# Layer 0's MLP in two passes over seven quarter products, with adaLN sums in batches of two column tiles

## The chip, the cores and the metric

The kernel runs on one core of one Trainium2 chip. The metric is the device time of one execution in microseconds (us), given as the median of three runs. The engines are named as in the profile: PE (TensorE, matmuls), DVE (VectorE), ACT (ScalarE), POOL (GpSimd) and SP (SyncE, which here only issues DMAs).

## The reference, cut to what matters

Two layers work on 1280 tokens (1024 of one sample, 256 of one prompt) of width 1024. Each layer is a mixer and then an MLP of hidden width 4096. Shift, scale and gate of every sub-layer come from a product of a conditioning vector with `ada_w` (adaLN), one vector for the sample and one for the prompt.

```python
for i in range(DEPTH):
    mod = (jax.nn.silu(cond) @ ada_w[i] + ada_b[i])[:, None, :]
    sh1, sc1, g1, sh2, sc2, g2 = jnp.split(mod, 6, axis=-1)
    h = _rms_norm(x, norm_mix[i]) * (1.0 + sc1) + sh1
    ...
    x = x + g1 * out
    h = _rms_norm(x, norm_mlp[i]) * (1.0 + sc2) + sh2
    x = x + g2 * (jnp.square(jax.nn.relu(h @ mlp_w1[i])) @ mlp_w2[i])
return _rms_norm(x, final_norm), jnp.stack(states, axis=1)
```

The mixer of layer 0 is a gated MLP over chunks beside a retention in two directions; that of layer 1 pools over windows of the sequence. The chunks of hidden columns, the passes and the quarter products below are the kernel's, the reference has only the two products.

## The kernel before

**Layout.** Activations lie transposed: 128 features on the partitions, 8 feature tiles (`DT`), 1280 tokens along the free axis in three blocks of 512, 512 and 256 (`TB`; the last is the prompt). `X` is the residual, `hH`/`hL` (layer 0) and `h1H`/`h1L` (layer 1) the normalized input of an MLP. Every operand of a product is held as a high and a low half, and `pair_pass` (L527) issues three matmuls for one product: high by high, high by low, low by high. The three matmuls of one 128 by 128 weight tile with a block of 512 tokens are called x512 below, those with the 256 tokens of the prompt or 256 columns x256, and counts are of single matmuls.

**Weights.** The hidden width is cut into 16 chunks (`NCH`) of 256 columns (`UC`). SP loads 1 MB of weights into `stage`, ACT rounds it to the high half in one of two places of `ring` (L933), POOL subtracts to get the low half (L1516). `stage` holds one load, so a next load waits for both.

**Layer 0's MLP** keeps `X` in SBUF. A chunk does its w1 product, squares the ReLU of it and adds its w2 product to `X` at once. `mlp(0, 0, first=True)` and `mlp(0, 15, last=True)` do so with plain products. Chunks 1 to 14 are a loop over `mlp_fast` (PE L2842, ACT L1247, POOL L1620, DVE L2232): the w1 product is plain (six blocks, `first_product`), the w2 product of the 1024 sample tokens uses seven products of quarter matrices for eight (`second_product`, in the order `FAST_SEQ`), and the prompt's is plain.

**Layer 1's MLP** runs in two passes, and frees SBUF for them by storing `X` to DRAM. After `plain_chunk(0)` and `(1)`, `first_pass(s, c)` (PE L2990, ACT L1391, POOL L1688, DVE L2378) handles chunks 2 to 15, chunk `2s + c`: seven quarter products for the w1 product of the sample tokens, in the order A11·B11, A12·B21, S1·G1, S2·G2, prompt 0, S3·G3, prompt 1, A22·G4, S4·B22. `G1` to `G4` are sums of quarters of the input, made once; `S1` to `S4` are sums of quarters of the weights, made in each chunk by POOL (L1674 to L1684) and split into `qsH` (ACT L1363) and `qsL` (POOL L1662). DVE adds the products (L2386: names s11, s22, s12 in the code), squares the ReLU (L2392: B11, B22, B12; `midB` and `u` in the profile) and forms the mid sums T1, T3, T2, T4 (L2368 to L2376). SP stores all of it to `mid_spill`. Then `second_pass(s)` takes two chunks at a time, loads the stored units back, and does seven quarter products again for the w2 product; `last_second` does the last two chunks plainly and finishes the tokens.

**adaLN of layer 1.** Its product with the conditioning vectors is not done on PE but as scaled sums on DVE, in the chunks of layer 0's MLP. Chunk `ch` takes batch `ch` of 16 batches; a batch has three column tiles: a load of 1.5 MB into `ada_st_mlp` (L666), and 16 DVE instructions of 128x384 (`ada_part`, L1855; two multiplications L1869, then fourteen multiply-and-adds L1872 whose two tensor inputs are the loaded tile and the running sum, both in SBUF). In the loop they come in four parts between the squares of the first blocks. In the next chunk PE transposes the sums (`ada_of_chunk`, L2767, three matmuls twice), and DVE reduces the result to columns of `mod` (L2172). While these parts run in the loop, POOL has nothing to do: its work for a chunk (weight sums L1626 to L1635, low halves) lies before and after.

**What sets the order.** Each engine's program is written out by hand, and each waits on semaphores for counts of the others'. An engine takes its instructions strictly in order; the DMA issues are in order on SP.

Of the kernel before, what the change touches and what calls it, by code (L numbers as in the profile page):

```python
# [119 lines left out]
FACTORS = {1: ("A11", "B11"), 2: ("A12", "B21"), 3: ("S4", "B22"), 4: ("A22", "T4"), 5: ("S1", "T1"), 6: ("S2", "T2"),  # L120
           7: ("S3", "T3")}
GOES_TO = {1: (0, 0), 2: (0, 0), 6: (0, 1), 5: (1, 1), 7: (1, 1), 3: (0, 1), 4: (1, 0)}
CHAIN = {6: 1, 7: 6, 4: 7, 3: 5}
FAST_SEQ = ([(1, d) for d in range(HD)] + [(2, d) for d in range(HD)]
            + [(p, d) for d0 in range(0, HD, 2) for p in (6, 5, 7, 3, 4) for d in (d0, d0 + 1)] + [("prompt", d) for d in range(DT)])
FAST_GRP = len(FAST_SEQ)
FAST_BANK = [(2, 3, 6, 1, 4, 5, 2, 3)[d] if p == "prompt" else (6, 1)[d % 2] if p in (2, 3, 5) else 2 + d for p, d in FAST_SEQ]
FAST_TILE = [(2, d) if p == "prompt" else (GOES_TO[p][1], HD * GOES_TO[p][0] + d) for p, d in FAST_SEQ]
FIRST_BANK = (0, 1, 0, 0, 0, 0)
LO_ORDER = ["B11", "B21", "T1", "T2", "B22", "T3", "T4", "p0", "p1"]  # L130
FAST_MID = len(LO_ORDER)


def earlier(seq, n):

    return max([i for i in range(n) if seq[i] == seq[n]], default=-1)


def products(l, ch):

    if not isinstance(ch, int):
        return FAST_GRP * ch + (GRP - FAST_GRP) if len(FAST[l]) else GRP * ch
    return GRP * ch + (FAST_GRP - GRP) * sum(1 for c in FAST[l] if c < ch)


def halves(l, ch):

    if not isinstance(ch, int):
        return FAST_MID * ch + (PAIRS - FAST_MID) if len(FAST[l]) else PAIRS * ch
    return PAIRS * ch + (FAST_MID - PAIRS) * sum(1 for c in FAST[l] if c < ch)  # L150


ADDS = {}
for _t, _d in BY_BLOCK:
    if _d > 0:
        ADDS[(_t, _d)] = len(ADDS)

# [2997 lines left out]
```

## Time and profile before

| | us |
|---|---|
| median of 3 runs | 2457.58 (2453.61 to 2458.58) |
| the profiled execution | 2457.45 |
| its span (first to last instruction) | 2455.5 |
| PE busy in it | 2400.2 (98%) |
| DVE busy | 1594.6 (65%) |
| POOL busy | 987.3 (40%) |
| ACT busy | 792.0 (32%) |
| mean granted TensorE clock | 0.996 of full |

Layer 0's mixer takes the first 680 us, layer 0's MLP lies from about 684 to 1511 us, layer 1's mixer up to about 1649, its MLP up to the end. In the lists of the profile a timeline row gives the start, the time of the whole row, the engine, the line, the operation with its output and inputs, how many instructions it stands for, and in brackets the idle time before and what ended it. Single matmuls are shown with their full latency (0.39 us for 512 columns) though they are issued closer together, so the pace is read from the distance of two starts.

### The profile page before, as it was taken

How to read it: one execution, taken by the hardware profiler on the slowest of the kernel's cores; microseconds unless marked ns; L12 is line 12 of the kernel's file. 1: busy time of each engine (PE TensorE's matmuls, PEld its weight loads, DVE VectorE, ACT ScalarE, POOL GpSimd, SP SyncE). 2: the span in 40 equal slices, each digit the busy share in tenths (PEclk: the TensorE clock that was granted, in tenths of full speed). 3: DMA queues.
4: the chain of work that ended last, by engine and by line, in shares of the span. 5: the costliest groups of instructions: out<-in, count | busy, mean ns of one | idle time of the engine just before them, and what ended most of it. 6: DMA issues, size and time to landing. Idle time of an engine off the chain costs nothing.

```text
span 2455.5 us, 37931 instructions
## 1 busy us (share of the span) xinstructions
PE 2400.2 (98%) x13516; PEld 2088.5 (85%) x13516; DVE 1594.6 (65%) x2600; ACT 792.0 (32%) x1234; POOL 987.3 (40%) x520
## 2 busy tenths in 40 slices
PE   8999999989999999999999999899999999999998
PEld 5988889988878888888888888778888888888887
DVE  6666832285487878877877886578333327877764
ACT  4311112151332223223223222764333334333322
POOL 0135321173023333333333333036656667776740
PEclk9999999999999999999999999999999999999999
DMA  8334523384212111221211131033343355343322
GB/s 294 121 130 153 150 91 110 121 283 157 78 60 78 60 60 60 73 89 63 74 60 60 60 102 35 18 116 124 108 141 116 132 177 217 131 146 125 121 86 86
DMA packets 156705, 274.07 MB, mean 112 GB/s; under 512 B 7716, under 2 KB 103752, under 8 KB 155720
## 3 DMA queue, kind: packets, MB, share of 16 engines
q1 hardware_dynamic: 149200, 263.22, 31.2%
q10 hardware_dynamic: 7416, 9.63, 1.4%
q8 instruction: 60, 0.98, 0.2%
q14 instruction: 29, 0.24, 0.0%
HBM read 204.66 MB, written 63.96 MB: 109 GB/s over the span
## 4 chain that ended last, share of the span: by engine, by line
PE 87%; DVE 7%; ACT 2%; issue 2%; POOL 1%; DMA 1%; SPq 0%; DVEq 0%; ACTq 0%; POOLq 0%
PE bank L527 83%; PE bank L2687 1%; PE bank L2577 1%; DMA hL_f<-in_ada_w_dram 1%; ACT yn L1136 1%; DVE X L1880 1%; DVE rst L2048 1%; DVE ada_acc_in L1872 0%; PE bank L2774 0%; DVE G1L L2357 0%; DVE ada_acc_mlp L1872 0%; DVE xgm L2080 0%; ACT pF L1186 0%; DVE h1L L2087 0%; PE bank L2636 0%
## 5 line engine op out<-in xcount | busy, mean ns | idle before, releaser
L1880 DVE SCALAR_TENSOR_TENSOR X<-bank,mod,X 128x512 f32<-128x512 f32 (+1 forms) x852 | 544.9, 683 | 232.7 <-PE bank L527 232.4
L527 PE MATMUL bank<-hH,ring 128*128 128x512 f32 (+1 forms) x2496 | 686.8, 357 | 0.5 <-DVE hL L2087 0.5
L1516 POOL TENSOR_TENSOR ring<-stage,ring 128x2048 fp32r<-128x2048 f32 x64 | 304.9, 4764 | 587.7 <-ACT ring L933 587.7
L527 PEld LDWEIGHTS bank<-hH,ring 128*128 128x128 f32 x2496 | 445.0, 189 | 66.6 <-DVE hL L2087 1.6
L527 PE MATMUL bank<-hL,ring 128*128 128x512 f32 (+1 forms) x1248 | 441.9, 354 | 0.0
L527 PEld LDWEIGHTS bank<-hL,ring 128*128 128x128 f32 x1248 | 236.2, 189 | 32.2
L527 PE MATMUL bank<-ring,hH 128*128 128x256 f32 (+1 forms) x1024 | 224.4, 315 | 3.7 <-POOL ring L1516 3.3
L933 ACT ACTIVATE ring<-stage 128x2048 fp32r<-128x2048 f32 x65 | 124.1, 1909 | 302.1 <-PE bank L527 289.8
L527 PE MATMUL bank<-midH,ring 128*128 128x256 f32 (+1 forms) x864 | 214.0, 329 | 4.3 <-DVE X L1880 4.3
L527 PE MATMUL bank<-h1H,ring 128*128 128x256 f32 (+1 forms) x864 | 209.4, 327 | 1.0 <-DVE h1L L2087 0.6
L527 PEld LDWEIGHTS bank<-ring,hH 128*128 128x128 f32 x1024 | 168.2, 192 | 15.3 <-issue 3.9
L2386 DVE TENSOR_TENSOR u<-u,bank 128x512 f32<-128x512 f32 x42 | 28.9, 688 | 213.9 <-PE bank L527 212.9
L527 PEld LDWEIGHTS bank<-midH,ring 128*128 128x128 f32 x864 | 148.3, 192 | 19.1 <-DVE X L1880 5.2
L527 PEld LDWEIGHTS bank<-h1H,ring 128*128 128x128 f32 x864 | 148.1, 190 | 17.2 <-DVE h1L L2087 1.8
L527 PE MATMUL bank<-ring,hL 128*128 128x256 f32 (+1 forms) x512 | 159.5, 312 | 0.0
L1872 DVE SCALAR_TENSOR_TENSOR ada_acc_mlp<-ada_st_mlp,sc,ada_acc_mlp 128x384 f32<-128x384 f32 (+1 forms) x266 | 149.7, 629 | 0.0
L1635 POOL TENSOR_TENSOR sumL<-sumF,sumH 128x2048 fp32r<-128x2048 f32 x14 | 64.6, 4616 | 204.2 <-DVE midF L2270 204.2
L527 PE MATMUL bank<-midL,ring 128*128 128x256 f32 (+1 forms) x432 | 141.9, 329 | 0.0
L527 PE MATMUL bank<-h1L,ring 128*128 128x256 f32 (+1 forms) x432 | 141.0, 326 | 0.0
L1699 POOL TENSOR_TENSOR ring<-stage,ring 128x1024 fp32r<-128x1024 f32 x32 | 82.9, 2601 | 56.2 <-ACT ring L1378 55.6
L527 PEld LDWEIGHTS bank<-ring,hL 128*128 128x128 f32 x512 | 98.3, 192 | 5.2
L1872 DVE SCALAR_TENSOR_TENSOR ada_acc_in<-ada_st_in,sc,ada_acc_in 128x384 f32<-128x384 f32 x112 | 98.4, 946 | 0.0
(382 smaller groups left out, 4833.6 us busy)
## 6 DMA issues: line engine op xcount, KB each, us to landing
stage<-in_mlp_w_dram SPq DMA_DIRECT2D x64, 1024.0 KB, 5.5
ada_st_mlp<-in_ada_w_dram SPq DMA_DIRECT2D x18, 1536.0 KB, 8.2
stage<-in_ev_w_in_dram SPq DMA_DIRECT2D x14, 1024.0 KB, 5.2
mid_spill<-midT SPq DMA_DIRECT2D x56, 256.0 KB, 2.2
ada_st_in<-in_ada_w_dram SPq DMA_DIRECT2D x8, 1536.0 KB, 7.2
mid_spill<-midB SPq DMA_DIRECT2D x48, 256.0 KB, 2.0
gt<-gate_spill SPq DMA_DIRECT2D x20, 256.0 KB, 3.9
x_spill<-X SPq DMA_DIRECT2D x2, 2560.0 KB, 10.5
```

The costliest lines, as they stand in the source:

```text
L527: mm = nc.tensor.matmul(out, a, b, start=first and n == 0, stop=last and n == 2, skip_group_check=chained)
L933: nc.scalar.activation(ringH[slot][:, :], stage[:, :], ACT.Copy).then_inc(w_hi, 1)
L1136: ev = nc.scalar.activation(yn[n % 2][:, d, h, :], bank[2 + 2 * (n % 2) + d][:, h * P:(h + 1) * P], ACT.Identity, scale=rmv[n % 2][:, j, 1 ...
L1516: nc.gpsimd.tensor_tensor(ringL[slot][:, :], stage[:, :], ringH[slot][:, :].bitcast(F32), ALU.subtract).then_inc(w_lo, 1)
L1635: nc.gpsimd.tensor_tensor(sumL[:, :, :], sumF[:, :, :], sumH[:, :, :].bitcast(F32), ALU.subtract).then_inc(s_lo[l], 1)
L1699: nc.gpsimd.tensor_tensor(rows_of(ringL[slot], part), rows_of(stages[c], part), rows_of(ringH[slot], part).bitcast(F32), ALU.subtract).the ...
L1872: V.scalar_tensor_tensor(out=acc, in0=src, scalar=sc2[:, k, cond:cond + 1], in1=acc, op0=ALU.mult, op1=ALU.add).then_inc(a_acc, 1)
L1880: V.scalar_tensor_tensor(out=X[:, d, cols(t)], in0=src[:, 0:TB[t][1]], scalar=gate_ap, in1=X[:, d, cols(t)], op0=ALU.mult, op1=ALU.add).th ...
L2048: e = V.bn_stats(rst[n % 2][:, HEADS * d + h, :], bank[2 + 2 * (n % 2) + d][:, h * P:(h + 1) * P])
L2386: V.tensor_tensor(buf[:, :], buf[:, :], src[:, :], ALU.add).then_inc(m_dve, 1)
L2577: mm = nc.tensor.matmul(bank[6 + d][:, h * P:(h + 1) * P], kx[j % 2][:, d, h, :], val[:, n, h * P:(h + 1) * P], start=True, stop=True)
L2687: mm = nc.tensor.transpose(tile_pair(q, j)[:, d * P:(d + 1) * P], X[:, d, n * P:(n + 1) * P], ident)
```

## The change

- Layer 0's MLP gets the structure of layer 1's: `mlp(l)` is now one function on each engine and called for both layers. `X` goes to DRAM (`x_kept`, 5 MB in two stores) and back; squared units are stored and loaded; both products use seven quarter products. In PE's program the MLP of layer 0 has 2904 x512 and 1536 x256 matmuls before, 2736 and 1536 after. The number of transposes for the sums is 96 in both.
- The inputs `B11` to `T4` of layer 0's second pass take the place of `hH`/`hL` in SBUF.
- The sums for layer 1's adaLN become 24 batches of two column tiles (1 MB, 16 DVE instructions of 128x256 each), two for each of the chunks 2 to 13. Batch `a` = 2ch−4 stands on DVE between B11 and s22, batch `b` = 2ch−3 between B22 and s12. There is one buffer for the loads, `ada_pair_st`, so a load waits for the sums of the batch before. PE turns `a` in the same chunk ahead of prompt product 1, and `b` in the next chunk ahead of S1·G1.
- POOL's program of a first-pass chunk in layer 0 is that of layer 1: weight sums, low halves, the subtractions for S1 to S4.
- Band tables and the low half of the pooling weight (`pool_weights`) are made on POOL after layer 0's last mid product; the weight has a buffer of its own.
- The tokens of layer 0's last blocks go through other SBUF places (`tile_at`), and one of them (tile 4) is turned and normalized a step earlier (`LAST_MM_AT`, `LAST_RS_AT`, `LAST_LO_AT`).

```diff
-            UA, n0, h0, p0 = U_MLP[l] + 2 * ch, PAIRS * ch, halves(l, ch), products(l, ch)
...
-        mlp(0, 0, first=True)
-        with pe.Fori(1, NCH - 1) as ch:
-            mlp_fast(0, ch)
-        mlp(0, NCH - 1, last=True)
...
+        def ada_pair_load(b):
+
+            sp.wait_ge(a_acc, ADA_OPS * (BATCHES_L0 + b))
+            sp.dma_start(ada_pair_st[:, :, :], ada_v[1][:, :, bass.ds(ADA_TILES * P * b, ADA_TILES * P)]).then_inc(a_raw, 16)
...
+            def first_stores(s, c):
+
+                ch = 2 * s + c
+                sp.wait_ge(m_dve, first_dve(l, ch) + D_AT["B11"])
+                mid_store(s, c, "B11", "B11")
+                if l == 0 and not closing(s):
+                    ada_pair_load(2 * ch - 3)
+                sp.wait_ge(m_dve, first_dve(l, ch) + D_AT["B22"])
+                mid_store(s, c, "B22", "B22")
+                if not closing(s):
+                    w1_load(ch + 2)
...
+        def ada_pair(b):
+
+            n = BATCHES_L0 + b
+            dve.wait_ge(a_raw, 16 * n + 16)
+            dve.wait_ge(a_mm, 2 * BATCHES_L0 + b)
+            for i in range(ADA_OPS):
+                k, cond = divmod(i, 2)
+                acc, src = ada_pair_acc[cond][:, :, :], ada_pair_st[:, k, :].rearrange("p (j n) -> p j n", j=ADA_TILES)
+                if k == 0:
+                    V.tensor_scalar(acc, src, sc2[:, k, cond:cond + 1], None, ALU.mult).then_inc(a_acc, 1)
+                else:
+                    dve.wait_ge(a_acc, ADA_OPS * n + i - 1)
+                    V.scalar_tensor_tensor(out=acc, in0=src, scalar=sc2[:, k, cond:cond + 1], in1=acc,
+                                           op0=ALU.mult, op1=ALU.add).then_inc(a_acc, 1)
...
+                total("s11", u1, bank[1], "2", "u1")
+                relu_squared("B11", u1)
+                if turned is not None:
+                    ada_pair_columns(turned, 1)
+                if first is not None:
+                    ada_pair(first)
+                total("s22", u5, bank[0], "7", "u5")
+                relu_squared("B22", u5)
+                if first is not None:
+                    ada_pair_columns(first, 0)
+                    ada_pair(first + 1)
...
+                total("s12", u2, bank[2], "3", "u2")
+                relu_squared("B12", u2)
...
+                quarter_product(bank[0][:, :], "S3", "G3", False)
+                if first is not None:
+                    ada_pair_turn(first, 0)
+                prompt_product(1)
+                pe.wait_ge(m_dve, d0 + D_AT["s22"])
+                quarter_product(bank[0][:, :], "A22", "G4", False)
```

**DVE.** Before, in the loop over layer 0's chunks, the sums stand between squares of the ReLU (L2237) and their low halves (L2242):

```order
L2172 TENSOR_REDUCE mod<-bank 128x3
...
L1869 TENSOR_SCALAR ada_acc_mlp<-ada_st_mlp,sc_164 128x3x128 x2
L1871 ISA
L1872 SCALAR_TENSOR_TENSOR ada_acc_mlp<-ada_st_mlp,sc_164,ada_acc_mlp 128x3x128
L1871 REGISTER_ALU
...
L2237 TENSOR_TENSOR relu_188<-relu_188 128x512
L2241 REGISTER_ALU
L2242 TENSOR_TENSOR midL<-relu_188,midH 128x512
```

After, in the first chunk of the first pass (chunk 2): the end of batch `a`, then s22 and B22, the columns, batch `b`, s12 and B12, and the mid sums:

```order
L2099 SCALAR_TENSOR_TENSOR ada_pair_acc_229<-ada_pair_st,sc_141,ada_pair_acc_229 128x256
L2189 TENSOR_TENSOR u_185<-u_185,bank 128x512
L2195 SCALAR_TENSOR_TENSOR midB_178<-u_185 128x512
L2107 TENSOR_REDUCE mod<-bank 128x2 x2
L2096 TENSOR_SCALAR ada_pair_acc_228<-ada_pair_st,sc_141 128x256
L2096 TENSOR_SCALAR ada_pair_acc_229<-ada_pair_st,sc_141 128x256
...
L2099 SCALAR_TENSOR_TENSOR ada_pair_acc_229<-ada_pair_st,sc_141,ada_pair_acc_229 128x256
L2189 TENSOR_TENSOR u_186<-u_186,bank 128x512
L2195 SCALAR_TENSOR_TENSOR u_186<-u_186 128x512
L2171 TENSOR_TENSOR midT_179<-u_186,midB_177 128x512
```

A whole batch of sums now stands ahead of s22, and another ahead of s12 and the mid sums.

**PE.** Before, the transposes of a chunk's sums stand ahead of the w1 product's first two blocks:

```order
L2905 ISA
L2769 ISA
L2774 MATMUL bank<-csm,ada_acc_mlp 128x128 x3
L2876 REGISTER_ALU
L527 MATMUL bank<-hH,ring 128x512
L527 MATMUL bank<-hL,ring 128x512
```

After, those of batch `a` stand between S3·G3 and prompt product 1 of the same chunk:

```order
L532 MATMUL bank<-G3H,hH 128x512
L532 MATMUL bank<-G3L,hH 128x512
L532 MATMUL bank<-G3H,hL 128x512
L2635 MATMUL bank<-csm,ada_pair_acc_228 128x128 x2
L2635 MATMUL bank<-csm,ada_pair_acc_229 128x128 x2
L532 MATMUL bank<-hH,ring 128x256
L532 MATMUL bank<-hL,ring 128x256
```

The turn moved from the chunk after the sums into the chunk of the sums.

**SP.** Before, the DMA issues of a chunk in layer 0's loop:

```order
L666 ISA
L666 DMA ada_st_mlp<-in_ada_w_dram 128x8x384
L253 ISA
L642 ISA
L642 DMA stage<-in_mlp_w_dram 128x8x256
L253 REGISTER_ALU
L642 ISA
L642 DMA stage<-in_mlp_w_dram 128x2x1024
```

After, those of a first-pass chunk of layer 0 (stores of units, two loads for the sums, one of weights):

```order
L805 DMA mid_spill<-midB_177 128x512
L668 ISA
L669 ISA
L669 DMA ada_pair_st<-in_ada_w_dram 128x8x256
...
L805 DMA mid_spill<-midB_178 128x512
...
L811 DMA stage<-in_mlp_w_dram 128x8x256
...
L805 DMA mid_spill<-midp 128x512
...
L805 DMA mid_spill<-midB_182 128x512
...
L669 DMA ada_pair_st<-in_ada_w_dram 128x8x256
```

The load for batch `b` (L669, its wait L668) now stands ahead of the weight load, and the one for the next chunk's batch `a` after the store of B21.

## Rows read from the trace of the kernel before

**Rows 1.** Windows: one chunk of layer 0's loop, one of layer 1's first pass.

```profile
core 0: us, PE busy (x) PEld busy (x) DVE busy (x) ACT busy (x) POOL busy (x), PEclk, DMA share, GB/s
845.57:898.67 53.10, 53.10 (x284) 45.91 (x283) 41.69 (x71) 15.09 (x21) 18.95 (x7) 1.00 0.21 69
1756.48:1781.32 24.84, 24.84 (x133) 21.52 (x133) 8.54 (x10) 8.75 (x15) 15.15 (x10) 1.00 0.37 127
```

**Rows 2.** Chain in layer 0's chunk loop: start us, us, instruction, count.

```profile
838.75 0.33 PE bank L2774 x3
839.08 5.49 PE bank L527 x24
```

**Rows 3.** Timeline, PE in chunk 0 of layer 0: start us, us, instruction, count [idle before].

```profile
719.02 0.39 PE L527 MATMUL bank<-midL,ring 128*128 128x512 f32 x1
...
719.70 0.39 PE L527 MATMUL bank<-midL,ring 128*128 128x512 f32 x1
```

**Rows 4.** Timeline, DVE in a chunk of layer 1's first pass.

```profile
1742.70 0.69 DVE L2392 SCALAR_TENSOR_TENSOR midB<-u 128x512 f32<-128x512 f32 x1
1753.04 0.69 DVE L2386 TENSOR_TENSOR u<-u,bank 128x512 f32<-128x512 f32 x1 [9.64 <-PE bank L527]
1753.76 1.38 DVE L2392 SCALAR_TENSOR_TENSOR midB<-u 128x512 f32<-128x512 f32 x1
1761.38 0.69 DVE L2386 TENSOR_TENSOR u<-u,bank 128x512 f32<-128x512 f32 x1 [6.23 <-PE bank L527]
1762.10 1.81 DVE L2392 SCALAR_TENSOR_TENSOR u<-u 128x512 f32<-128x512 f32 x1
...
1766.03 0.69 DVE L2376 TENSOR_TENSOR midT<-midB,midT 128x512 f32<-128x512 f32 x1
```

**Rows 5.** Two-tile sums, a reduction (DVE), a 1 MB load (DMA view, last figure us to landing).

```profile
17.51 5.62 DVE L1893 SCALAR_TENSOR_TENSOR ada_sum<-X,sc,ada_sum 128x256 f32<-128x256 f32 x14
L1810 DVE TENSOR_REDUCE mod<-bank 128x2 f32<-128x256 f32 x2 | 0.8, 418 | 0.0
ada_st_mlp<-in_ada_w_dram SPq DMA_DIRECT2D x1, 1024.0 KB, 5.1
```

**Rows 6.** Timeline, POOL in the chunk of rows 4.

```profile
1753.30 1.30 POOL L1682 TENSOR_TENSOR qsF<-stage 128x512 f32<-128x512 f32 x1
1754.54 1.76 POOL L1684 TENSOR_TENSOR s<-stage,qsF 128x512 f32<-128x512 f32 x1
1756.26 3.79 POOL L1662 TENSOR_TENSOR qsL<-qsF,qsH 128x512 fp32r<-128x512 f32 x3
...
1762.08 1.28 POOL L1662 TENSOR_TENSOR qsL<-s,qsH 128x512 fp32r<-128x512 f32 x1 [2.03 <-ACT qsH L1363]
```

**Rows 7.** Timeline, DVE and POOL in the mixing stage of layer 0.

```profile
334.03 11.85 DVE L1872 SCALAR_TENSOR_TENSOR ada_acc_in<-ada_st_in,sc,ada_acc_in 128x384 f32<-128x384 f32 x14
333.97 4.62 POOL L1516 TENSOR_TENSOR ring<-stage,ring 128x2048 fp32r<-128x2048 f32 x1 [36.73 <-ACT ring L933]
...
353.91 7.49 DVE L1872 SCALAR_TENSOR_TENSOR ada_acc_in<-ada_st_in,sc,ada_acc_in 128x384 f32<-128x384 f32 x14
356.90 8.88 POOL L1516 TENSOR_TENSOR ring<-stage,ring 128x2048 fp32r<-128x2048 f32 x1 [18.31 <-ACT ring L933]
```

**Rows 8.** Timeline, POOL beside the sums of a chunk of layer 0's loop.

```profile
1125.51 4.62 POOL L1635 TENSOR_TENSOR sumL<-sumF,sumH 128x2048 fp32r<-128x2048 f32 x1 [14.59 <-DVE midF L2270]
```

**Rows 9.** Timeline, POOL: first and last piece of the band tables.

```profile
1485.74 0.70 POOL L1585 MEMSET bandT<- 128x144 f32 x4
...
1497.89 0.10 POOL L1612 MEMSET band_edge<- 128x1 f32 x1
```

**Rows 10.** Waits of PE over the whole span: total us, times, longest us.

```profile
PE bank L527 <- DVE X L1880: 5.1, 4, 2.3
PE bank L527 <- POOL ring L1699: 2.1, 1, 2.1
PE bank L527 <- DVE G4L L2357: 2.0, 1, 2.0
```

**Rows 11.** Timeline of PE, and window, at the end of layer 0's MLP.

```profile
1509.37 0.39 PE L527 MATMUL bank<-midH,ring 128*128 128x256 f32 x1 [2.26 <-DVE X L1880]
1509.00:1513.00 4.00, 3.63 (x18) 3.63 (x19) 2.46 (x6) 0.00 (x0) 4.00 (x1) 0.59 0.00 0
```

More of the change, by code:

```diff
@@ L112 @@
 END_DVE_AT = {10: [0], 12: [1], 14: [2], 16: [3], 18: [4], 20: [5], 21: [6], 23: [7, 8, 9]}
-FAST = [range(1, NCH - 1), range(0)]
 HD = DT // 2
[L120 to L156, printed above, removed]
 SLOT_END = NT - 2
@@ L373, in build @@
     cd = small("cd", [P, 8])
+    dead_kb = off[0]
     vmv = small("vmv", [P, NT * 4, 2])
@@ new lines, in build, with held @@
+    F_KB = {"B11": 0, "p": 8, "B21": 40, "T2": 48, "T1": 24, "T3": 32, "B22": 64, "T4": 72}
+    QUARTER = {"B11": (0, 0, 0), "p": (0, 1, 0), "B21": (1, 0, 0), "T2": (1, 1, 0), "T1": (0, 1, 1), "B22": (1, 1, 1)}
+    def held(name, full, i):
+        m = ((hH_f, hL_f) if full else (hH, hL))[1 if name == "T4" else 0 if name == "T3" else QUARTER[name][0]]
+        if name in ("T3", "T4"):
+            return m[:, HD * i:HD * (i + 1), 1024:T]
+        _, half, tb = QUARTER[name]
+        return m[:, HD * half + 2 * i:HD * half + 2 * i + 2, 512 * tb:512 * (tb + 1)]
@@ L1492, in _ @@
-        for i in (1, 2, 3, 4):
-            sum2_hi(0, i, (1,))
-        mid_high(0, "T1")
-        mid_high(0, "T3")
-        second_pass(0)
-        with act.Fori(1, NSUP - 2) as s:
-            second_pass(s)
-        second_pass(NSUP - 2, plain=True)
-        act.wait_ge(m2_mm[1], M2_END)
-        w2_high(NSUP - 1, 0, 1)
-        w2_high(NSUP - 1, 1, 1)
-        mid_high(NSUP - 1, "B22")
+        mlp(1)
         for j in range(NT):
@@ L1770, in _ @@
[L1770 to L1777 removed]
+        mlp(1)
     @block.vector
@@ L2452, in _ @@
-        mid_low(0, "T2")
-        second_pass(0)
-        with dve.Fori(1, NSUP - 2) as s:
-            second_pass(s)
-        second_pass(NSUP - 2, plain=True)
-        mid_low(NSUP - 1, "T1", 3)
-        mid_low(NSUP - 1, "B22", 4)
+        mlp(1)
         for i, (t, d) in enumerate(BY_LAST):
@@ L2647, in _ @@
                     (state_keys, state_values)[half_of](ADVANCE[n])
-            if ui - 1 in ADA_IN_UNITS and ui < FIRST_GATE and not (kind == "u" and half == 1):
+            if ui - 1 in ADA_IN_UNITS and ui <= VAL_FIRST and not (kind == "u" and half == 1):
                 if ui == 5:
@@ L2720, in pool_tile @@
             else:
-                pe.wait_ge(gain_ok, 6) if j else pe.wait_ge(relu_ok[0], NTB * HT * NCH)
+                after(pe, gain_ok, 6 if j else 0)
             tile_in(2, j)
```

1771 lines of the change are left out of this document (766 added, 1005 removed).

## The prediction

> **What bounds the kernel now.** I looked first at PE, which is busy for 98% of the span, and then at the two stages that the change concerns, by windows. In one chunk of layer 0's loop PE is busy for all of the 53.10 us, and in one chunk of layer 1's first pass for all of its 24.84 us [rows 1]. So today both stages run at PE's pace, and whatever PE no longer issues is gained, as long as DVE and POOL keep up. How much room they have is in the same rows: in layer 1's chunk DVE is busy for 8.54 us and POOL for 15.15. The sums of adaLN are what has to be fitted in there. The reader is to see in the DVE rows of that chunk the two gaps in which they will lie: 9.64 us ahead of s22 and 6.23 us ahead of s12, both waits for PE [rows 4].
>
> **What is removed.** PE issues 2904 − 2736 = 168 matmuls of 512 columns fewer. Three of them take 719.70 − 719.02 = 0.68 us [rows 3], 0.2267 us each, so 168 are 38.1 us. The x256 and the transposes stay the same in number. The loop of before gives nothing more back, since PE has no idle time in it [rows 1]. If PE bounds everything in the new layer 0 too, the time is 2457.45 − 38.1 = 2419.4 us.
>
> **The pace of PE in the new chunk.** The first pass of layer 0 has layer 1's matmuls (24.84 us) and twice four transposes. Three transposes take 839.08 − 838.75 = 0.33 us [rows 2], eight 0.88. So PE alone would need 24.84 + 0.88 = 25.7 us for each of the 12 chunks with sums.
>
> **The chain on DVE.** A multiply-and-add of 128x256 takes 5.62 / 14 = 0.40 us [rows 5], a batch of 16 is 6.4 us. There is one buffer, so the load of batch b starts only when a's sums have read it: 5.1 us to landing for 1 MB [rows 5], and I add an estimated 0.5 us for SP to notice and DVE to go on, 5.6 in all. s22, B22 and two reductions lie under it (0.69 + 0.69 + 2 × 0.42 = 2.2 us [rows 4, 5]). One round of the chunk is then: s11 and B11 1.4; two reductions 0.8; batch a 6.4; load of b 5.6; batch b 6.4; s12, B12 and four mid sums 4.2 (from 1761.38 to 1766.72 are 5.34 us, of which B12 took 1.12 longer than the 0.69 of B11 [rows 4]). The sum is 24.8 us, just under PE's 25.7. The next chunk's batch a has 6.4 us for its load, enough for 5.6. If DVE were alone, the sums would thus cost PE nothing.
>
> **What POOL adds.** DVE is not alone. The rows of layer 1's chunk show B22 at 1.38 us and B12 at 1.81 where B11 takes 0.69 [rows 4], each beside a subtraction on POOL that began just before or with it, and POOL's L1684 takes 1.76 where its like takes 1.30 [rows 6]. In layer 0's mixing stage it is clearer: fourteen multiply-and-adds that take 7.49 us in one place take 11.85 beside one POOL instruction of 4.62, that is 4.4 longer; and a POOL instruction that starts inside the 7.49 takes 8.88 instead of 4.62, 4.3 longer [rows 7]. So a DVE instruction with two inputs in SBUF and a POOL instruction do not run together, they add up. DVE instructions that read PSUM (L2386, 0.69 in every row) are not held up. The loop of before kept out of this: POOL is idle for 14.59 us around the sums [rows 8]. The new place does not: POOL has its work in every first-pass chunk, and the sums are at both of its halves.
>
> So I add up what cannot overlap in one chunk. DVE: 28 multiply-and-adds × 0.40 = 11.2; B11, B22, B12 2.1; four mid sums 2.6 (the 5.34 us above without s12, B12 and the wait behind it); together 15.9. (The four multiplications, with one SBUF tensor, I count as free.) POOL: 15.15 less the hindrance of 0.46 in L1684 = 14.7 [rows 1, 6]. The sum is **30.6 us** against PE's 25.7: this is the lower bound, if POOL is packed into every moment that DVE leaves free. The upper one follows from where those moments are. Of DVE's 24.8 us, 8.9 are free, but most in pieces of 0.7 to 0.8 us (s11, s22, s12, reductions, multiplications), shorter than any POOL instruction of 1.3; only the load's 5.6 us less B22 is a long one. If POOL gets only these 4.9 us, the chunk takes 24.8 + 14.7 − 4.9 = **34.6 us**. I take 33.0, nearer to the upper end, because a POOL instruction that overhangs a short piece holds DVE for its rest, and because PE's own waits leave some time unused by both.
>
> The page "SBUF — State Buffer" of the Trainium skill ("Who interferes with whom") has the same as a rule: a DVE instruction with two SBUF inputs and a GpSimd instruction that reads SBUF need one shared port, and who starts first holds it for the whole instruction. By it alone POOL would get in between any two of DVE's, and the chunk would be near 34.6. The row with 8.88 us speaks against that half of it, since there a stream of DVE instructions held POOL off until its end; by this the chunk would be near 30.6.
>
> The stall is thus 33.0 − 25.7 = 7.3 us in each of 12 chunks, **+88 us**. It shows at PE's turn of batch a, ahead of prompt product 1. Queued behind DVE's sums are s22, B22, s12 and the mid sums, and for those wait A22·G4 and the next S1·G1 on PE, the stores and the weight load on SP. Chunks 14 and 15 have no sums and keep 24.84.
>
> **The rest of the change.** The stores and loads of X and units are those of layer 1, whose chunk has a DMA share of 0.37 [rows 1]; with 2 MB for the sums I expect no DMA bound: from 0 to +5 us. The second pass is a copy of layer 1's: its start there costs PE waits of 2.0 and 2.1 us [rows 10], and these come; the wait of 2.26 at the end of layer 0's MLP [rows 11] and one for X goes (5.1 us in four, 2.3 the longest [rows 10]). I count 0, from −4 to +4. The band tables take 1498.0 − 1485.74 = 12.3 us of POOL [rows 9]. They now come after POOL's last mid product, after the last split of weights, while PE has the plain closing products of layer 0: 192 x512, 192 × 0.2267 = 43.5 us. That is their cover; half of them uncovered would be +6, so 0, up to +6. Tile 4 a step earlier is 0 to −1.
>
> **Sum.** 2457.45 − 38.1 + 88 + 0 = **2507 us**. The profiled execution (2457.45, its span 2455.5 and 2 us around it) is practically the median of the runs (2457.58).
>
> **Rivals.**
> *A, the other side: DVE and POOL fit.* Mechanism: POOL's instructions fall into DVE's free 8.9 us and DVE's into POOL's pauses, or the interference binds less with 0.40 us instructions than with those I read. The chunk stays at PE's 25.7 and the time is 2419; each us above costs 12. It decides at a chunk of 25.7 + 38.1 / 12 = 28.9 us: below, the change wins. For it: mid sums and sums of 128x256 without POOL beside them run unhindered. Against: the bound of 30.6 is only arithmetic on what rows 7 show. Chance 0.17, of it 0.13 below 2450.
> *B, packed.* Streams of DVE hold POOL off, and POOL catches up in the load and in PE's time. 30.6 us, stall 4.9 × 12 = 59, time 2478. Chance 0.28.
> *C, alternating and slower still.* 34.6 us, 8.9 × 12 = 107, time 2526; and PE's pauses may cost clock: after one of 2.26 us the window shows a granted clock of 0.59, about half of 2.4 GHz for most of 4 us [rows 11]. Such a window costs about 0.41 × 4 = 1.6 us, in 12 chunks 20 us, if PE has no slack behind the turn: 2546. Chance 0.20.
> *D, not what it says.* PE's second pass of layer 0 waits for loads or splits, or the load of b is late on SP behind the store of B11: up to some 2 us in each of 7 rounds beside any of the others. Chance 0.03 by itself.
> My forecast between B and C has 0.32.
>
> A page of the Trainium skill, "TensorE: Matmul & The Clock Gate" (Why this matters for your kernels), has it that idle gaps between bursts of matmuls bring the half rate; the row with 0.59 agrees, and that is the second half of rival C.
>
> **The numbers.** Range: A beyond its upper part (0.13) and the far end of C (0.05) are left out, so from 2440 to 2545. A measurement of this kernel can tell about 0.2% (5 us) from no change. Faster than 2452.5: 0.15. Within: 0.05. Slower: 0.80.
>
> **What the profile after would show.** Matmuls of `pair_pass` fewer by 168. Distance between SP's weight loads in layer 0's first pass: 33 us (25.7 by A, 30.6 by B, 34.6 by C). Idle time of PE of about 7 us before the first transposes of each chunk, released by the sums, and next to none there by A. The mean of a two-tile multiply-and-add well above 0.48 us, and POOL's L1674 to L1684 and L1516 of layer 1's kind longer in layer 0 than in layer 1. Layer 0's second pass at the pace of layer 1's. I would be wrong if the multiply-and-adds show their 0.48 beside busy POOL rows, or if PE waits for something else than the sums.

## The result

The changed kernel takes 2544.49 us (median of 4 runs, 2540.73 to 2546.89), the one before 2455.92 in the same comparison. The ratio is 1.036, with an interval from 1.0341 to 1.0379. That is 88.6 us slower. The forecast was 2507 in a range from 2440 to 2545, so the direction and the mechanism were right and the loss was 1.8 times the one forecast (49.6). The median lies 0.5 us inside the range and two of the four runs lie above it, so that the range held is luck. The profiled execution has a span of 2539.0 us, and its mean granted clock fell from 0.996 to 0.974.

The pace of layer 0's first pass is read from SP's weight loads, one for each chunk (timeline of SP after the change, start and duration in us first):

```profile
862.48 0.41 SPq L811 DMA_DIRECT2D stage<-in_mlp_w_dram  x1
...
899.21 0.41 SPq L811 DMA_DIRECT2D stage<-in_mlp_w_dram  x1
...
936.25 0.41 SPq L811 DMA_DIRECT2D stage<-in_mlp_w_dram  x1
```

The three stand 36.73 and 37.04 us apart; over 12 chunks, from 717.98 to 1154.52 us, the mean is 36.38. PE alone needs 25.72, as a run below shows. Where PE waits, over the whole span of the changed kernel:

```profile
PE bank L2635 <- DVE ada_pair_acc L2099: 96.1, 11, 10.8
...
PE bank L532 <- DVE u L2189: 9.3, 1, 9.3
```

96.1 us are waits ahead of the turn of batch a, in 11 places (8.7 us each), that is in every chunk with sums but the first. Each looks like this one in PE's timeline:

```profile
897.24 1.09 PE L2635 MATMUL bank<-csm,ada_pair_acc 128*128 128x128 f32 x4 [8.40 <-DVE ada_pair_acc L2099]
```

The forecast said to look at DVE and POOL beside each other. First DVE in one chunk of the changed kernel's first pass (the batch a before it ends at 896.9; 903.29 is b, 916.99 is the next a):

```profile
896.92 0.67 DVE L2189 TENSOR_TENSOR u<-u,bank 128x512 f32<-128x512 f32 x1
...
902.76 0.62 DVE L2096 TENSOR_SCALAR ada_pair_acc<-ada_pair_st,sc 128x256 f32<-128x256 f32 x2 [3.50 <-DMA ada_pair_st<-in_ada_w_dram]
903.29 5.63 DVE L2099 SCALAR_TENSOR_TENSOR ada_pair_acc<-ada_pair_st,sc,ada_pair_acc 128x256 f32<-128x256 f32 x14
909.03 0.69 DVE L2189 TENSOR_TENSOR u<-u,bank 128x512 f32<-128x512 f32 x1
909.75 1.81 DVE L2195 SCALAR_TENSOR_TENSOR u<-u 128x512 f32<-128x512 f32 x1
...
916.99 17.08 DVE L2099 SCALAR_TENSOR_TENSOR ada_pair_acc<-ada_pair_st,sc,ada_pair_acc 128x256 f32<-128x256 f32 x14
933.99 0.67 DVE L2189 TENSOR_TENSOR u<-u,bank 128x512 f32<-128x512 f32 x1
```

Then POOL in the same stretch:

```profile
909.73 1.29 POOL L1565 TENSOR_TENSOR hL<-s,hH 128x512 fp32r<-128x512 f32 x1 [13.01 <-ACT hH L1253]
917.62 1.39 POOL L1577 TENSOR_TENSOR hL_f<-stage 128x512 f32<-128x512 f32 x1 [6.61 <-PE bank L532]
920.44 1.59 POOL L1581 TENSOR_TENSOR hL_f<-hL_f,stage 128x512 f32<-128x512 f32 x1 [1.43 <-PE bank L532]
921.99 4.79 POOL L1451 TENSOR_TENSOR ring<-stage,ring 128x2048 fp32r<-128x2048 f32 x1
926.73 1.45 POOL L1585 TENSOR_TENSOR hL_f<-stage 128x512 f32<-128x512 f32 x1
928.14 1.44 POOL L1587 TENSOR_TENSOR s<-stage,hL_f 128x512 f32<-128x512 f32 x1
929.55 4.25 POOL L1565 TENSOR_TENSOR hL<-hL_f,hH 128x512 fp32r<-128x512 f32 x3
```

The reader is to see three things. Batch b takes 5.63 us for its fourteen multiply-and-adds, the 0.40 each of [rows 5]. Batch a takes **17.08** for the same fourteen. And POOL has nearly its whole work of the chunk, eight of nine instructions, from 917.62 to 933.80, inside batch a; it is idle under the load of b (896.92 to 902.76) and under batch b.

The first chunk with sums shows the same program with another timing. There PE came late to S1·G1 (the 9.3 us of wait for s11 above), so POOL's block, which waits for that product, was released only when most of batch a was done. The batch takes 5.63 us, and PE has no wait at its turn (DVE's and POOL's timeline):

```profile
739.05 5.63 DVE L2099 SCALAR_TENSOR_TENSOR ada_pair_acc<-ada_pair_st,sc,ada_pair_acc 128x256 f32<-128x256 f32 x14
743.08 2.75 POOL L1577 TENSOR_TENSOR hL_f<-stage 128x512 f32<-128x512 f32 x1 [6.77 <-PE bank L532]
```

Windows of the changed kernel: behind the turn, a whole chunk, and layer 0's second pass.

```profile
899.00:903.00 4.00, 4.00 (x20) 4.00 (x20) 0.51 (x2) 0.00 (x0) 0.00 (x0) 0.50 1.02 349
899.21:936.25 37.04, 28.61 (x141) 24.89 (x141) 32.81 (x47) 8.75 (x14) 16.03 (x9) 0.87 0.41 141
1180.00:1500.00 320.00, 317.88 (x1707) 276.01 (x1706) 232.33 (x264) 115.80 (x142) 227.40 (x131) 1.00 0.44 156
```

The clock is 0.50 behind PE's pause, the chunk has PE busy for 28.61 of 37.04 us (against 24.84 of 24.84 in [rows 1]), and the second pass runs at PE's pace with 317.88 of 320.

### The profile page after: what moved, and what is told of

It is laid out like the page before. It is cut to its first block, busy times and chain, and to the rows that moved or that the text cites. A ratio compares the mean times of both kernels' runs of the same rounds, so it can differ in the third digit from the quotient of the medians.

```text
span 2539.0 us, 37580 instructions
## 1 busy us (share of the span) xinstructions
PE 2386.4 (94%) x13348; PEld 2078.1 (82%) x13348; DVE 1665.8 (66%) x2457; ACT 836.9 (33%) x1299; POOL 1211.5 (48%) x702
## 3 DMA queue, kind: packets, MB, share of 16 engines
q1 hardware_dynamic: 196128, 337.68, 38.1%
## 4 chain that ended last, share of the span: by engine, by line
PE 78%; DVE 10%; issue 8%; ACT 2%; DMA 1%; POOL 1%; SPq 0%; DVEq 0%; ACTq 0%; POOLq 0%
PE bank L532 73%; DVE ada_pair_acc L2099 2%; PE bank L2548 1%; DVE G1L L2160 1%; PE bank L2436 1%; PE bank L2845 1%; DMA hL_f<-in_ada_w_dram 1%; DVE G1F L2137 1%; ACT yn L1151 1%; POOL ring L1602 1%; DVE rst L1967 0%; PE bank L2635 0%; DVE G3F L2140 0%; DVE xgm L1999 0%; DVE h1L L2006 0%
## 5 line engine op out<-in xcount | busy, mean ns | idle before, releaser
L532 PE MATMUL bank<-hH,ring 128*128 128x256 f32 (+1 forms) x2856 | 650.6, 337 | 4.2 <-POOL ring L1602 3.0
L1799 DVE SCALAR_TENSOR_TENSOR X<-bank,mod,X 128x512 f32<-128x512 f32 (+1 forms) x576 | 373.9, 686 | 280.0 <-PE bank L532 277.9
L1451 POOL TENSOR_TENSOR ring<-stage,ring 128x2048 fp32r<-128x2048 f32 x47 | 223.7, 4759 | 289.0 <-ACT ring L946 289.0
L2099 DVE SCALAR_TENSOR_TENSOR ada_pair_acc<-ada_pair_st,sc,ada_pair_acc 128x256 f32<-128x256 f32 x336 | 263.1, 856 | 0.0
L1602 POOL TENSOR_TENSOR ring<-stage,ring 128x1024 fp32r<-128x1024 f32 x64 | 166.0, 2609 | 110.0 <-ACT ring L1268 109.6
L532 PEld LDWEIGHTS bank<-h1H,ring 128*128 128x128 f32 x864 | 148.1, 190 | 17.2 <-DVE h1L L2006 1.8
L1268 ACT ACTIVATE ring<-stage 128x1024 fp32r<-128x1024 f32 x64 | 65.8, 1055 | 220.0 <-DMA stage<-in_mlp_w_dram 181.7
L1622 POOL TENSOR_TENSOR qsL<-qsF,qsH 128x512 fp32r<-128x512 f32 x83 | 127.0, 1555 | 0.0
L1257 ACT ACTIVATE u<-bank 128x512 f32<-128x512 f32 x84 | 50.3, 599 | 205.1 <-PE bank L532 201.6
L946 ACT ACTIVATE ring<-stage 128x2048 fp32r<-128x2048 f32 x48 | 91.7, 1910 | 63.6 <-PE bank L532 51.6
L2635 PE MATMUL bank<-csm,ada_pair_acc 128*128 128x128 f32 x96 | 19.8, 343 | 96.1 <-DVE ada_pair_acc L2099 96.1
L1614 POOL TENSOR_TENSOR qsF<-stage 128x512 f32<-128x512 f32 x42 | 77.3, 1853 | 59.4 <-PE bank L532 59.4
```

The source lines that it names most:

```text
L532: mm = nc.tensor.matmul(out, a, b, start=first and n == 0, stop=last and n == 2, skip_group_check=chained)
L946: nc.scalar.activation(ringH[slot][:, :], stage[:, :], ACT.Copy).then_inc(w_hi, 1)
L1257: nc.scalar.activation(dst[:, :], src[:, :], ACT.Copy).then_inc(m_act, 1)
L1268: nc.scalar.activation(rows_of(ringH[(U_MLP[l] + c) % 2], part), rows_of(stages[c], part), ACT.Copy).then_inc(w_hi, 1)
L1451: nc.gpsimd.tensor_tensor(ringL[slot][:, :], stage[:, :], ringH[slot][:, :].bitcast(F32), ALU.subtract).then_inc(w_lo, 1)
L1602: nc.gpsimd.tensor_tensor(rows_of(ringL[slot], part), rows_of(stages[c], part), rows_of(ringH[slot], part).bitcast(F32), ALU.subtract).the ...
```

## The experiments

The changed kernel is the base of all but the last. The kernel before was run beside each group on the same chip; its medians there lie between 2452.6 and 2458.4 us. The theory throughout is that batch a is held up by POOL's instructions, because each of its multiply-and-adds has both tensor inputs in SBUF. POOL's instructions beside it read SBUF too, and no run changes that side.

**Running sums in PSUM.** No multiply-and-add has two SBUF inputs any more; all else stays.

```diff
+                part = bank[6][:, 2 * P * cond:2 * P * (cond + 1)].rearrange("p (j n) -> p j n", j=ADA_TILES)
                 if k == 0:
-                    V.tensor_scalar(acc, src, sc2[:, k, cond:cond + 1], None, ALU.mult).then_inc(a_acc, 1)
+                    V.tensor_scalar(part, src, sc2[:, k, cond:cond + 1], None, ALU.mult).then_inc(a_acc, 1)
...
-                    V.scalar_tensor_tensor(out=acc, in0=src, scalar=sc2[:, k, cond:cond + 1], in1=acc,
+                    V.scalar_tensor_tensor(out=acc if k == DT - 1 else part, in0=src, scalar=sc2[:, k, cond:cond + 1], in1=part,
```

> The changed kernel, but the running sums of the two-tile batches lie in a free PSUM bank, and only the last of the eight steps writes them to SBUF. So no multiply-and-add has two inputs in SBUF; their number, shape, place and loads are the same. Theory (a batch that runs beside POOL's work is held up by exclusion of two-input SBUF instructions): batch a falls from 17 us to about 6, the chunk of 37.0 us to PE's 25.7, the time by 11.3 x 12 = 136 to about 2410-2425. Rival (the sums' own volume and their single buffer are the chain): the chunk stays near 37 us, 2544.

Measured: 2420.3 us, ratio to before 0.9855 (0.9835 to 0.9876). The loss is gone, and the kernel is faster than both. DVE and POOL in one chunk of this kernel, and the window of a chunk:

```profile
897.05 4.79 DVE L2100 SCALAR_TENSOR_TENSOR bank<-ada_pair_st,sc,bank 128x256 f32<-128x256 f32 x12
901.75 0.86 DVE L2100 SCALAR_TENSOR_TENSOR ada_pair_acc<-ada_pair_st,sc,bank 128x256 f32<-128x256 f32 x2
905.83 0.69 DVE L2190 TENSOR_TENSOR u<-u,bank 128x512 f32<-128x512 f32 x1 [3.22 <-PE bank L532]
...
909.30 4.79 DVE L2100 SCALAR_TENSOR_TENSOR bank<-ada_pair_st,sc,bank 128x256 f32<-128x256 f32 x12
```

```profile
897.44 1.29 POOL L1577 TENSOR_TENSOR hL_f<-stage 128x512 f32<-128x512 f32 x1 [6.61 <-PE bank L532]
...
901.52 4.61 POOL L1451 TENSOR_TENSOR ring<-stage,ring 128x2048 fp32r<-128x2048 f32 x1
...
909.05 3.79 POOL L1565 TENSOR_TENSOR hL<-hL_f,hH 128x512 fp32r<-128x512 f32 x3
```

```profile
909.29:935.01 25.72, 25.72 (x141) 22.27 (x140) 22.07 (x47) 8.70 (x15) 15.11 (x10) 1.00 0.61 203
```

Batch a, 4.79 and 0.86 us, overlaps with POOL's instructions of 897.44 and 901.52, and batch b (909.30) with the three of 909.05; none of them is longer for it. PE is busy for all of the 25.72 us of the chunk. So it was neither the amount of the sums nor their single buffer. The gap of 3.22 us ahead of s22 is DVE waiting for PE again.

**PSUM for one batch only.** With `part = acc if odd else bank[6]...` for the first of the two, and reversed for the second.

> Running sums in PSUM for the first batch of each chunk only (a, between B11 and s22); the second (b) keeps them in SBUF as in the changed kernel. Theory: all of the loss is made in batch a (17.08 us; b takes 5.63), so about the time with both in PSUM, 2420, at most +5. Rival (any two-input batch loses, since POOL's work moves to the other place when it is free in the first): b now takes up POOL's instructions and the time stays above 2450.

> The reverse: only the second batch of each chunk (b) has its running sums in PSUM. Theory: b was never held up (5.63 us), so nothing changes: 2544, within 5. Rival as for the reverse: part of the gain, 2480.

Measured: a in PSUM 2428.0 us (0.9894, 0.9863 to 0.9925); b in PSUM 2541.1 (1.0356, 1.0323 to 1.0389). All but 8 us of the loss is batch a's. The 8 us, more than the 5 allowed, are the rival's remainder. The intervals of this kernel and of the one with both batches in PSUM overlap; in the traces the distance of SP's weight loads after the first chunk is 26.31 us here and 25.76 there, which makes 6 us. DVE's and POOL's timeline with a in PSUM:

```profile
913.36 1.65 DVE L2097 TENSOR_SCALAR ada_pair_acc<-ada_pair_st,sc 128x256 f32<-128x256 f32 x2 [1.60 <-DMA ada_pair_st<-in_ada_w_dram]
914.94 7.69 DVE L2100 SCALAR_TENSOR_TENSOR ada_pair_acc<-ada_pair_st,sc,ada_pair_acc 128x256 f32<-128x256 f32 x14
```

```profile
892.70 3.65 POOL L1565 TENSOR_TENSOR hL<-s,hH 128x512 fp32r<-128x512 f32 x1 [3.47 <-ACT hH L1253]
...
912.22 3.94 POOL L1565 TENSOR_TENSOR hL<-hL_f,hH 128x512 fp32r<-128x512 f32 x3
918.46 1.50 POOL L1565 TENSOR_TENSOR hL<-s,hH 128x512 fp32r<-128x512 f32 x1 [2.30 <-ACT hH L1253]
```

Now that a is out of POOL's way, the end of POOL's work (912.22) reaches into batch b: its two multiplications take 1.65 us for 0.62, its multiply-and-adds 7.69 for 5.63. The first POOL row shows the other side: started inside a batch b, an instruction of 1.3 us takes 3.65, until that batch has ended. In the next chunk the same instruction (918.46) got in at once and took 1.50. The first met a batch that had run undisturbed for 3.1 us, the second one that POOL had interrupted 2.3 us before; whether that decides it was not tested.

**Half of POOL's subtraction.** Its share of the low halves of w1 in layer 0's first pass covers 1024 of 2048 columns; the rest is left out.

```diff
-                split_lo(U_MLP[l] + ch, (U_MLP[l] + c) % 2)
+                if l == 0 and m0 is not None:
+                    slot, half = (U_MLP[l] + c) % 2, slice(0, 1024)
+                    pool.wait_ge(w_hi, U_MLP[l] + ch + 1)
+                    nc.gpsimd.tensor_tensor(ringL[slot][:, half], stage[:, half], ringH[slot][:, half].bitcast(F32),
+                                            ALU.subtract).then_inc(w_lo, 1)
```

> The changed kernel, but in layer 0's first pass POOL's subtraction for the low half of the weights (4.79 us in the chunk looked at) covers only half of its columns; the rest of the low halves is left out. Theory: POOL's 2.4 us less inside batch a are 2.4 us less for the chunk, 12 x 2.4 = 29 us, about 2516. Rival (POOL's work is not on the path, the sums are slow by themselves or by DMA): no change, 2544.

Measured: 2489.3 us (1.0141, 1.0117 to 1.0164), 55 us less than the changed kernel, about twice what was expected. One batch a on DVE, and POOL's end beside it:

```profile
903.24 11.88 DVE L2105 SCALAR_TENSOR_TENSOR ada_pair_acc<-ada_pair_st,sc,ada_pair_acc 128x256 f32<-128x256 f32 x14
```

```profile
907.85 2.59 POOL L1585 TENSOR_TENSOR ring<-stage,ring 128x1024 fp32r<-128x1024 f32 x1
...
914.80 4.37 POOL L1565 TENSOR_TENSOR hL<-hL_f,hH 128x512 fp32r<-128x512 f32 x3
```

Batch a is 11.88 us, 5.2 less and not 2.2. The row of three subtractions (914.80) now starts as the batch ends: since the batch is shorter, it is over before POOL's last instructions come.

**The same work in four instructions.** POOL's 128x2048 as four of 128x512, nothing left out.

```diff
-                split_lo(U_MLP[l] + ch, (U_MLP[l] + c) % 2)
...
+                    for i in range(4):
+                        part = slice(512 * i, 512 * (i + 1))
+                        e = nc.gpsimd.tensor_tensor(ringL[slot][:, part], stage[:, part], ringH[slot][:, part].bitcast(F32), ALU.subtract)
+                    e.then_inc(w_lo, 1)
```

> The changed kernel, but in layer 0's first pass POOL's subtraction of 128x2048 (4.79 us) is issued as four of 128x512. If DVE and POOL add up by their durations, as the forecast had it, the time stays (2544, or some us more for three more instruction starts). If they take turns one by one, DVE gets three more multiply-and-adds of 0.4 us through while POOL works: 12 x 1.2 = 14 us less, about 2530.

Measured: 2512.6 us (1.0239, 1.0207 to 1.0271), 32 us less, for the same work on both engines. Against the expectation of taking turns (14 less) it is over twice that. One batch a, and POOL beside it:

```profile
942.97 13.82 DVE L2107 SCALAR_TENSOR_TENSOR ada_pair_acc<-ada_pair_st,sc,ada_pair_acc 128x256 f32<-128x256 f32 x14
```

```profile
943.60 1.39 POOL L1577 TENSOR_TENSOR hL_f<-stage 128x512 f32<-128x512 f32 x1 [6.60 <-PE bank L532]
946.42 1.59 POOL L1581 TENSOR_TENSOR hL_f<-hL_f,stage 128x512 f32<-128x512 f32 x1 [1.43 <-PE bank L532]
947.97 5.73 POOL L1587 TENSOR_TENSOR ring<-stage,ring 128x512 fp32r<-128x512 f32 x4
953.66 1.44 POOL L1593 TENSOR_TENSOR hL_f<-stage 128x512 f32<-128x512 f32 x1
955.07 1.44 POOL L1595 TENSOR_TENSOR s<-stage,hL_f 128x512 f32<-128x512 f32 x1
956.47 4.38 POOL L1565 TENSOR_TENSOR hL<-hL_f,hH 128x512 fp32r<-128x512 f32 x3
```

Here the pattern can be counted. While both have work, POOL's instructions of 128x512 follow each other at 1.43 us (5.73 for four) and DVE gets one multiply-and-add of 0.40 through with each. The changed kernel shows this turn-taking in a single row: beside POOL's instruction of 921.99 one multiply-and-add, and no more, is on DVE (its timeline cut to 923 to 924 us):

```profile
922.24 4.82 DVE L2099 SCALAR_TENSOR_TENSOR ada_pair_acc<-ada_pair_st,sc,ada_pair_acc 128x256 f32<-128x256 f32 x1
```

So each POOL instruction of 128x512 costs DVE 1.43 − 0.40 = 1.03 us. In this batch there are eight (1.39, 1.59, four, 1.44, 1.44): 5.63 + 8 × 1.03 = 13.9, measured 13.82. After them DVE is through, and the last three find the batch gone. In the changed kernel the long one costs 4.79 − 0.40 = 4.4 and seven others 1.03 each: 5.63 + 4.4 + 7.2 = 17.2, measured 17.08. In four pieces the long one costs 4.1, nearly the same; the gain is that DVE has made its fourteen steps three pieces earlier and the last three, 3.1 us, fall out of the batch.

**PE kept busy; short loads; both.** 32 unused matmuls of 512 columns ahead of the turn of a. Loads of an eighth, so that the sums use old data for the rest. And the two together.

```diff
                 if first is not None:
+                    pe.wait_ge(a_col, 2 * BATCHES_L0 + first - 1)
+                    for i in range(32):
+                        nc.tensor.matmul(pair_bank(0)[:, :], hH[:, 4 + i % 4, 0:P], hH[:, i % 4, 0:512], start=True, stop=True)
                     ada_pair_turn(first, 0)
```

```diff
-            sp.dma_start(ada_pair_st[:, :, :], ada_v[1][:, :, bass.ds(ADA_TILES * P * b, ADA_TILES * P)]).then_inc(a_raw, 16)
+            ks = slice(0, DT if isinstance(b, int) and b == 0 else 1)
+            sp.dma_start(ada_pair_st[:, ks, :], ada_v[1][:, ks, bass.ds(ADA_TILES * P * b, ADA_TILES * P)]).then_inc(a_raw, 16)
```

> The changed kernel with 32 unused matmuls of 512 columns (7.3 us) on PE ahead of each turn of batch a, where PE idles for 8.4 us; the granted clock should stay at full rate behind the turn. If the half rate after the pause (0.50 in the window from 899 to 903 us) is on the path, the chunk gets shorter by up to 2 us, 24 us in all (2520). If DVE's chain alone sets the chunk, nothing changes (2544, within 5).

> The changed kernel, but all loads for the two-tile batches except the first move only an eighth (128 KB); the sums then use old data for the rest. Theory: the 5.6 us between the end of batch a and the start of b become about 2.7, so 2.9 x 12 = 35 us less, about 2509, and batch a stays at about 17 us. Rival (the sums are held up by the traffic of the loads): batch a falls towards 6 us and the time by 100 us or more.

> Both edits that did nothing alone, together: 32 unused matmuls keep PE busy ahead of the turn of batch a, and all loads for the batches but the first move an eighth. In the short-load run s12 no longer waited for DVE's batch b but for PE, 2.14 us, whose products behind the turn ran at half rate. If two chains of equal length (the load on DVE's side, PE at half rate on the other) meet at s12, taking both away shortens the chunk from 36.4 us by some 3 us: 12 x 3 = 36, about 2505-2510. If not, 2540 again.

Measured: busy PE 2541.4 us (1.0347, 1.0325 to 1.0369), short loads 2543.0 (1.0356, 1.0334 to 1.0377), both 2524.1 (1.0285, 1.0253 to 1.0317). With the busy PE the clock is up, in a window behind the turn:

```profile
901.00:905.00 4.00, 4.00 (x28) 3.67 (x27) 0.58 (x2) 0.80 (x2) 0.00 (x0) 1.00 0.97 327
```

but the time moves by 3 us only. A part of the gain is lost to the edit itself: in the first chunk PE has no pause, and the unused matmuls take 7.4 us there, so that the second distance of the weight loads is 39.28 us instead of 35.19. The ten distances after that have a mean of 35.77 us instead of 36.44. So the half rate alone costs about 0.7 us a chunk. With short loads (36.24 us in the same ten) DVE goes on at once and then waits for PE instead, and batch a is as long as ever, so the loads' traffic is not what holds it up:

```profile
899.27 0.62 DVE L2097 TENSOR_SCALAR ada_pair_acc<-ada_pair_st,sc 128x256 f32<-128x256 f32 x2
...
907.57 0.69 DVE L2190 TENSOR_TENSOR u<-u,bank 128x512 f32<-128x512 f32 x1 [2.14 <-PE bank L532]
...
915.54 17.06 DVE L2100 SCALAR_TENSOR_TENSOR ada_pair_acc<-ada_pair_st,sc,ada_pair_acc 128x256 f32<-128x256 f32 x14
```

The expected 35 us were wrong, since I had left out who comes next. Two chains run from the end of batch a to s12 and are equally long: on DVE the load and batch b (896.92 to 909.03, 12.1 us), on PE the turn, prompt product 1, A22·G4 and S4·B22 (897.24 to 908.9), of which the turn and prompt product 1 run at half the clock: the prompt's 24 matmuls take 5.27 us from 897.97, while those of prompt product 0 take 2.88. (In the short-load run s12 could start at 907.57.) With both taken away, the ten distances have a mean of 34.32 us, 2.1 less, where the two edits alone gave 0.7 and 0.2:

```profile
904.94 0.69 DVE L2190 TENSOR_TENSOR u<-u,bank 128x512 f32<-128x512 f32 x1 [0.75 <-PE bank L532]
```

In the whole kernel that is 20 us, less than the 36 expected. The load does not count with 5.6 us, since s22, B22 and the reductions lie under it; and PE is late by 0.75 us even at full clock.

**The start of the first pass.** On top of the sums in PSUM, DVE makes the mid sums of chunk 1 ahead of the low halves of G3 and of G4, and S1·G1 of chunk 2 waits for these alone.

```diff
             quarter_lo(1)
+            if l == 0:
+                dve.wait_ge(m_act, 12 * PLAIN)
+                mid_sums(0, 1, first_dve(l, 1))
             quarter_lo(2)
...
-                pe.wait_ge(m_dve, first_dve(l, ch - 1) + D_AT["s12"])
+                pe.wait_ge(m_dve, first_dve(l, ch - 1) + (4 if l == 0 and turned is None and first is not None else D_AT["s12"]))
```

> The kernel with all running sums in PSUM, with a second edit at the start of layer 0's first pass, where PE waits 9.28 us for s11 ahead of S1 x G1: the mid sums of chunk 1 stand on DVE ahead of the low halves of G3 and of G4 instead of behind them, and S1 x G1 of chunk 2 waits for the mid sums alone. Expected: the wait falls to 1-2 us and the time from 2420 to about 2413; if DVE's low halves of G3 and G4 then come too late for S3 x G3 and A22 x G4, the wait only moves and the time stays at 2420.

> The kernel with all running sums in PSUM once more, beside the one with the second edit on the same chip: 2420.

Measured: 2416.5 us (0.9835, 0.9813 to 0.9856) against 2422.1 (0.9851, 0.983 to 0.9872) for the PSUM kernel in the same group. The two intervals overlap, and so do the runs (2416.1 to 2420.0 against 2418.9 to 2423.4), so the 5.6 us are not clear of noise; the trace shows what was gained and what came instead:

```profile
728.97 0.50 PE L532 MATMUL bank<-G1H,hH 128*128 128x512 f32 x1 [0.59 <-DVE midT L2180]
...
735.45 0.79 PE L532 MATMUL bank<-G2H,hH 128*128 128x512 f32 x1 [3.47 <-ACT u L1257]
```

The wait of 9.28 us became 0.59 and 3.47. The second is for a copy on ACT that stands behind the high half of G4. By the medians that is 5.6 us of the 7 expected, and by the waits 5.2; it is the best median of the versions tried.

**A part that the forecast had not seen.** The kernel before with one piece of the change in layer 0's mixer: one turn of the sums later on PE, weights rounded earlier on ACT.

```diff
-                if ui in ALONE and g == (1 if ui >= FIRST_GATE else 0) or ui not in ALONE and ui - 1 not in ALONE and g == 0 and ui > 0:
+                if ui - 1 in ALONE and g == IN_GROUPS[ui] - 1 and ui + 1 < N_IN:
+                    split_static(ui + 2)
+                if 0 < ui <= 8 and g == 0:
                     split_static(ui + 1)
...
+                if step == 1:
+                    ada_total(ADA_IN_UNITS[8], 0)
...
-            if ui - 1 in ADA_IN_UNITS and ui < FIRST_GATE and not (kind == "u" and half == 1):
+            if ui - 1 in ADA_IN_UNITS and ui <= 8 and not (kind == "u" and half == 1):
```

> The kernel before with one part of the change alone, in layer 0's mixer: PE turns one batch of layer 0's sums two units later than before, and ACT rounds the following weights to their high half as soon as a place is free. In the trace of the changed kernel everything behind this place comes 8.8 us earlier, and PE's waits there of 2.32 us (for the sums) and 3.3 us (for POOL's low half) and the window with a clock of 0.72 behind them are gone. Theory: this part alone is worth 8 to 9 us: from 2456 to about 2447. Rival: the gain needs the rest of the change, 2456.

Measured: 2450.25 us against 2452.58, ratio 0.9985 (0.9973 to 0.9997). The chain of this kernel at the place has no waits:

```profile
334.90 14.52 PE bank L527 x121
349.42 0.66 PE bank L2477 x6
350.07 22.02 PE bank L527 x131
```

In the trace SP's last weight load ahead of layer 0's MLP comes at 676.56 us instead of 685.44. The medians, however, show 2.3 us, not 9. The kernel before has some runs from 2458 to 2462 us and the rest from 2449 to 2454, this one none above 2453.35. It may be that the kernel before meets this stall in some runs only, and in the profiled one it did; that is argued from the spread, not shown.

## Why the prediction was right, and where it was off

- **168 matmuls less, 38.1 us, and PE alone at 25.7 us a chunk.** Right. With the sums in PSUM the chunk is 25.72 us, and the kernel 2420.3, where rival A had 2419.4. That the two meet so closely is partly chance: the start of the first pass loses 11.1 us (36.81 for the first chunk instead of 25.7), the mixer gains, and neither was in the sum.
- **DVE and POOL do not run together, and the turn of batch a is where it shows.** Right. The waits are at this turn, 8.7 us each in the mean where I said about 7, and the mean of a two-tile multiply-and-add is 0.86 us over all 24 batches, where an undisturbed one has 0.48.
- **What adds up.** This is the term that was mis-sized: 33.0 us for a chunk, measured 36.38, so a stall of 10.7 us instead of 7.3. I had bounds of 30.6 and 34.6. The upper one was no bound. It let 4.9 us of POOL's work run under the load of batch b, the one long piece that DVE leaves free. POOL is idle there. Its work for a chunk waits for PE's products 5, 6 and 7 (S1·G1, S2·G2, S3·G3) and comes as a block, and this block lies in batch a, because PE does these products at that time; the first chunk, where they came later, has no hindrance in a. With nothing under the load the forecast's sum would be 24.8 + 14.7 = 39.5. That is too much, because DVE gets its 0.40 through with each POOL instruction, which the forecast had not. With the hindrances as measured it is 24.8 + 11.4 (in a) + 1.1 (in B12) = 37.3, measured 37.04 in the chunk shown. On PE's side the same chunk is 25.72 + 8.4 (the wait) + 2.9 (at the half rate) = 37.0. I had asked how much time DVE leaves free, and not when POOL's work is released.
- **Rows 7, one rule or the other.** The Trainium skill, "SBUF — State Buffer" ("Who interferes with whom"), has the shared port as an exclusive lock held for one instruction. In batch a the trace agrees: the engines take turns, 1.03 us for each short POOL instruction. In a batch b of the run with a in PSUM the other reading held: 3.65 us for a POOL instruction of 1.3, kept out until the stream ended, and in the changed kernel's first batch a too (2.75 us for 1.3). Both happen in this kernel; what decides between them was not settled.
- **The multiplications as free.** Wrong, though small: with one SBUF tensor they took 1.65 us for 0.62 beside POOL. With their output in PSUM they take 0.86 for two.
- **The clock (rival C).** The half rate came, 0.50 in the window behind the turn. It makes PE's own work 2.9 us longer in the chunk shown, but keeping PE busy gave back only 0.7 us a chunk; together with the load it is part of 20 us. My 20 us for it was a price for a chain without slack. The 2546 us of rival C, the nearest to the measured time, are thus no hit: its chunk of 34.6 was too short and its clock too dear, and the two errors met.
- **The rest counted as 0.** The sum for the profiled executions, read at the same weight load of SP in layer 1's first pass, 1731.64 us before and 1814.80 after: +83.2. It is made of −38.1 (matmuls), −8.0 (mixer, 685.44 to 677.49) and +128.1 (twelve chunks, 436.5 us less 12 × 25.7); these leave 1.2 for all else, loads, second pass, band tables and pooling. So those were right to be 0 in their sum. Two things were not seen. The edit in the mixer is one, its 8.0 us being open as said above. The other is the wait of 9.3 us for s11 at the start. In the changed kernel it costs nothing beyond the twelve chunks, since the first of them has this wait and none at its turn (36.95 us); in the kernel with the sums in PSUM it comes on top.

## What to carry to other kernels

When work is put on DVE beside POOL, ask not only how long both are busy but when each one's work is released, and lay the two side by side over one period: a stream with two SBUF inputs that meets a block of POOL instructions pays for the block, here 11.4 us on 5.6. If an accumulation's running sum can live in PSUM, its multiply-and-add costs the same (0.40 us for 128x256) and was nowhere held up by POOL here; it turned 3.6% slower into 1.5% faster. And where taking a wait away brings nothing, look for a second chain of the same length before giving up on it.
